# Two transformer blocks on one core: the order of products and adds in the second feed-forward, and the place of the modulation in the first

## The chip, the core and the metric

The kernel runs on one core of a Trainium2 chip. The metric is the device time of one execution in microseconds (us); where several executions were timed, their median. Engines are named as the profile names them: PE is TensorE (PEld its weight loads), DVE is VectorE, ACT is ScalarE, POOL is GpSimd, and SP is SyncE, which issues most of the DMAs.

## What is computed

A first transformer block (three kinds of attention, then a feed-forward) is followed by a second block whose two halves are modulated by a condition vector `c`. All tensors are float32, with 1024 tokens and a width of 1024. Of the reference these lines matter here:

```python
# first block, its second half
h = rmsnorm(x, g_mlp[l])
hid = jnp.square(jax.nn.relu(jnp.einsum("bsd,df->bsf", h, w_mlp_in[l])))
x = x + jnp.einsum("bsf,fd->bsd", hid, w_mlp_out[l])
# and, at its end, rmsnorm(x, g_final)

# second block
c_act = jax.nn.silu(c)
mod = c_act @ w_ada[l] + b_ada[l]                       # 1024 x 6144
sh1, sc1, gt1, sh2, sc2, gt2 = jnp.split(mod, 6, axis=-1)
h = _modulate(_rmsnorm(x, g_mix[l]), sh1, sc1)
x = x + gt1 * _mixer(h, ...)
h = _modulate(_rmsnorm(x, g_ffn[l]), sh2, sc2)
a = jnp.square(jax.nn.relu(jnp.einsum('bsd,df->bsf', h, w_ff1[l])))
x = x + gt2 * jnp.einsum('bsf,fd->bsd', a, w_ff2[l])
# and rmsnorm(x, g_final_2)
```

## The kernel before, in words

Each engine has its own program, written out by hand in the order in which it runs; semaphores join them. Nothing is scheduled by a planner. A float32 product is made of three matmuls on parts that were split into a high and a low half: high by high, high by low, low by high.

**The two feed-forwards.** The function `ff(0)` is the feed-forward of the first block and `ff(1)` that of the second; on each engine both are one piece of code, with `k` = 0 or 1. Each of the two matrix products of a feed-forward is done by a Strassen-Winograd scheme with seven half-size products, numbered 1 to 7.

- The **hidden phase** runs over the list `SEQ`: 16 units of the hidden width, seven products each, so 112 in all, each of twelve matmuls of 128x512 (PE lines 2523 to 2525). ACT splits the weights into their high part and DVE makes the low part (L1783), DVE also sums finished products (L1824), POOL makes the sums of weights and hidden tiles, and SP writes the finished hidden units to DRAM (`hidden_out`).
- The **output phase** runs over the list `STEPS`: 56 steps, 8 for each of the seven products in the order `ORDER2` = 1, 2, 5, 6, 3, 7, 4, with 24 matmuls a step (PE lines 2549 to 2551). For each step SP loads an operand from the hidden scratch (`a_load`) and one from the weights (`b_load`), ACT makes their high parts (L1245, L1250) and DVE their low parts (`step_lo`, L1931 and L1934) in rings of three buffers; for products 5, 6, 7 and 4 POOL first makes a difference of two weight tiles (`ff_b_sums`, L817). Products 1, 6, 7 and 4 add up in PSUM banks 0 to 3 and products 2, 5 and 3 in banks 4 to 7. One step after a product is complete, DVE's `evict` adds its four banks onto `xs`, the residual. In `ff(1)` each bank is first multiplied by the gate row `rowv` into `gained_sum` (L1885) and then added (L1889). PE waits, bank by bank, for the adds of a product before it writes its bank anew. From the loop's steps 3 to 10 SP also reloads `xs` from a scratch, one 512 KB piece a step; the last hidden unit is written at step 6 of SP's loop, and `a_load(7)` waits for that write to have landed, since it reads it back.

**The modulation** (`mod` above) is done beside the hidden phase of `ff(0)`. `w_ada` is cut into 96 "rows", pieces of 128x512 (256 KB). SP loads them in turn into two buffers `ada` (`ada_load`, L515), DVE multiplies each by a column of `c_act` and adds it into `ada_sum` (`modulation`, L1834 for the first of eight and L1836 for the other seven), and PE reduces every eight rows over partitions by four matmuls with a single column (`modulation`, L2490), into bank 4. The table `ADA_OPS` sets eight rows beside every eight products, from product 8 on. PE has one such group every eight products, from product 17 on: twelve in all. Since `ada_sum` is one tile, DVE's first row of a group waits for PE's matmuls on the group before. After the hidden phase DVE adds `b_ada` to the 48 columns (`modc`), makes the factors `1 + scale` (`amod`), and POOL writes 16 of the columns to a scratch (`mod_d`), from which two gate rows are read back later.

What the change touches: the table `ADA_OPS`; in the SP program `ff_loads`; in the POOL program `ff_b_sums`, the load of the row `g_final` into `rowv`, and the two writes to `mod_d`; in the DVE program `modulation`, `evict` and `ff`; in the PE program `modulation` and the loop over `STEPS` in `ff`.

## Time and profile before

| what | us |
|---|---|
| median of 3 executions (lowest, highest) | 2747.98 (2745.04, 2748.63) |
| profiled execution, its own time | 2745.53 |
| span of its trace | 2742.5 |
| PE busy | 2508.6 (91% of the span) |
| DVE busy | 1585.7 (58%) |
| ACT busy | 1214.5 (44%) |
| POOL busy | 837.7 (31%) |

The page gives the busy time of each engine and a granted TensorE clock, 0.966 of full speed as a mean over the span. Matmuls are pipelined: a row of PE shows a length of some 0.39 us, while one starts every 0.23 us, so times on PE are best read from starts. A row of the timeline is start, duration, engine, line, operation, what it writes from what it reads, the shape, and in brackets the idle time of that engine just before it with what ended it. In the rows and diffs below, `NS` is 56 and `NP` is 112.

### The profile page before, as it was taken

The page shows a single profiled execution, that of the slowest core. Times are in us where ns is not written, and L with a number is a line of the kernel's source. Part 1 is how long each engine was busy: PE and PEld are TensorE (multiplying, and loading weights), DVE is VectorE, ACT ScalarE, POOL GpSimd, SP SyncE. Part 2 cuts the span into 40 slices and gives each one's busy share as a digit, 9 for nine tenths or more (in the row PEclk, how much of TensorE's full clock was granted, in tenths as well). Part 3 has the DMA queues.
Part 4 walks back from the last instruction along what each step waited for, and adds up shares of the span by engine and source line. Part 5 has one row for each costly group of instructions (what it writes and reads, how often), then busy time and mean ns, then how long its engine had stood idle before and what let it go on. Part 6 is the DMA issues. An engine that isn't in the chain of part 4 may idle for free.

```text
span 2742.5 us, 32784 instructions
## 1 busy us (share of the span) xinstructions
PE 2508.6 (91%) x11852; PEld 2037.8 (74%) x11852; DVE 1585.7 (58%) x2796; ACT 1214.5 (44%) x2236; POOL 837.7 (31%) x740
## 2 busy tenths in 40 slices
PE   4997899997899799999999979988698999999997
PEld 4765778885678677777888867867586888877885
DVE  5357459875463787875545843335647444355675
ACT  6146357736312644444434443225426555543343
POOL 0222422231110355653333300004003655515142
PEclk9999999999999999999999989999798999999998
DMA  4102123334152267768755422122332444495444
GB/s 156 44 20 76 43 68 97 95 102 154 46 190 103 89 202 218 228 216 256 280 161 163 140 86 92 63 77 71 107 131 89 146 150 159 142 335 172 136 154 138
DMA packets 190128, 369.77 MB, mean 135 GB/s; under 512 B 13692, under 2 KB 58372, under 8 KB 189716
## 3 DMA queue, kind: packets, MB, share of 16 engines
q1 hardware_dynamic: 177620, 340.46, 37.8%
q10 hardware_dynamic: 8064, 14.68, 1.4%
q0 software_dynamic: 4288, 12.60, 1.4%
q8 instruction: 91, 1.49, 0.2%
q14 instruction: 65, 0.53, 0.1%
HBM read 266.95 MB, written 100.74 MB: 134 GB/s over the span
## 4 chain that ended last, share of the span: by engine, by line
PE 73%; DVE 11%; DMA 6%; ACT 5%; issue 3%; POOL 2%; SPq 0%; DVEq 0%; ACTq 0%; POOLq 0%
PE bank L2180 9%; PE bank L2181 9%; PE bank L2182 9%; PE bank L2549 7%; PE bank L2550 7%; PE bank L2551 7%; PE bank L2523 5%; PE bank L2525 5%; PE bank L2524 5%; DMA ada<-in_w_ada 3%; DVE ada_sum L1836 2%; PE bank L2357 1%; PE bank L2358 1%; PE bank L2359 1%; PE bank L2277 1%
## 5 line engine op out<-in xcount | busy, mean ns | idle before, releaser
L2523 PE MATMUL bank<-hq_hi,wq_hi 128*128 128x512 f32 x896 | 354.2, 395 | 17.6 <-DVE hq_lo L1844 11.1
L2549 PE MATMUL bank<-ring_b_hi,ring_a_hi 128*128 128x512 f32 x896 | 352.7, 394 | 13.6 <-DVE xs L1889 8.1
L2525 PE MATMUL bank<-hq_hi,wq_lo 128*128 128x512 f32 x896 | 352.4, 393 | 0.0
L2524 PE MATMUL bank<-hq_lo,wq_hi 128*128 128x512 f32 x896 | 352.0, 393 | 0.0
L2550 PE MATMUL bank<-ring_b_lo,ring_a_hi 128*128 128x512 f32 x896 | 351.5, 392 | 0.0
L2551 PE MATMUL bank<-ring_b_hi,ring_a_lo 128*128 128x512 f32 x896 | 351.3, 392 | 0.0
L1931 DVE TENSOR_TENSOR ring_a_lo<-a_raw,ring_a_hi 128x1024 fp32r<-128x1024 f32 x112 | 146.3, 1306 | 235.1 <-ACT ring_a_hi L1245 234.9
L1245 ACT ACTIVATE ring_a_hi<-a_raw 128x1024 fp32r<-128x1024 f32 x112 | 118.7, 1060 | 342.1 <-PE bank L2551 324.1
L2523 PEld LDWEIGHTS bank<-hq_hi,wq_hi 128*128 128x128 f32 x896 | 170.0, 190 | 58.0 <-DVE hq_lo L1844 16.5
L1783 DVE TENSOR_TENSOR wq_lo<-unit_raw,wq_hi 128x512 fp32r<-128x512 f32 x160 | 159.2, 1000 | 89.0 <-ACT wq_hi L1111 86.7
L2549 PEld LDWEIGHTS bank<-ring_b_hi,ring_a_hi 128*128 128x128 f32 x896 | 169.8, 189 | 53.8 <-DVE xs L1889 7.1
L2525 PEld LDWEIGHTS bank<-hq_hi,wq_lo 128*128 128x128 f32 x896 | 170.2, 190 | 36.2
L2551 PEld LDWEIGHTS bank<-ring_b_hi,ring_a_lo 128*128 128x128 f32 x896 | 169.9, 190 | 35.6
L2524 PEld LDWEIGHTS bank<-hq_lo,wq_hi 128*128 128x128 f32 x896 | 170.1, 190 | 34.9
L2550 PEld LDWEIGHTS bank<-ring_b_lo,ring_a_hi 128*128 128x128 f32 x896 | 169.9, 190 | 34.9
L1111 ACT ACTIVATE wq_hi<-unit_raw 128x512 fp32r<-128x512 f32 x160 | 99.7, 627 | 150.7 <-PE bank L2525 103.4
L817 POOL TENSOR_TENSOR chain_b<-b_raw,chain_b 128x1024 f32<-128x1024 f32 x32 | 92.0, 2876 | 215.8 <-DMA b_raw<-in_w_ff 115.9
L901 ACT ACTIVATE w_hi<-w_raw 128x512 fp32r<-128x512 f32 (+3 forms) x184 | 105.2, 604 | 98.6 <-DMA w_raw<-in_w_in 30.2
L722 POOL TENSOR_TENSOR w_lo<-w_raw,w_hi 128x512 fp32r<-128x512 f32 x56 | 74.8, 1344 | 227.4 <-ACT w_hi L901 223.1
L1418 DVE TENSOR_TENSOR w_lo<-w_raw,w_hi 128x512 fp32r<-128x512 f32 (+3 forms) x128 | 78.5, 649 | 88.9 <-ACT w_hi L901 87.3
L2180 PE MATMUL bank<-h_hi,w_hi 128*128 128x512 f32 (+1 forms) x288 | 113.3, 393 | 10.1 <-ACT qhT L1336 10.1
L1177 ACT ACTIVATE part<-bank 128x512 f32<-128x512 f32 x90 | 53.8, 598 | 154.2 <-PE bank L2525 154.2
(452 smaller groups left out, 5784.0 us busy)
## 6 DMA issues: line engine op xcount, KB each, us to landing
a_raw<-hidden_scratch SPq DMA_DIRECT2D x112, 512.0 KB, 3.4
hidden_scratch<-hidden SPq DMA_DIRECT2D x32, 1024.0 KB, 5.1
w_raw<-in_w_in SPq DMA_DIRECT2D x104, 256.0 KB, 2.8
ada<-in_w_ada SPq DMA_DIRECT2D x96, 256.0 KB, 3.0
hidden_scratch<-hidden SPq DMA_DIRECT2D x32, 768.0 KB, 4.8
unit_raw<-in_w_mlp_in SPq DMA_DIRECT2D x16, 1024.0 KB, 8.4
b_raw<-in_w_mlp_out SPq DMA_DIRECT2D x32, 512.0 KB, 4.6
unit_raw<-in_w_ff SPq DMA_DIRECT2D x16, 1024.0 KB, 5.3
```

The costliest lines, as they stand in the source:

```text
L1245: A_(ra_hi[s % 3][:, :, :], a_raw[raw_slot(s)][:, :, :], ACT.Copy).then_inc(a_hi.sem, 1)
L1783: tt(wq[p][1][:, :, :], unit_operand(p, u), wq[p][0][:, :, :].bitcast(f32), ALU.subtract).then_inc(wq_lo.sem, 1)
L1931: tt(ra_lo[r][:, :, :], a_raw[raw_slot(s)][:, :, :], ra_hi[r][:, :, :].bitcast(f32), ALU.subtract)\
L2180: mm(out, lh, rh, start=(i == 0), stop=False)
L2181: mm(out, lh, rl, start=False, stop=False)
L2182: last = mm(out, ll, rh, start=False, stop=(i == n - 1))
L2523: mm(o, lh[:, q, :], rh[:, q, :], start=(fresh and q == 0), stop=False, skip_group_check=True)
L2524: mm(o, lh[:, q, :], rl[:, q, :], start=False, stop=False, skip_group_check=True)
L2525: l = mm(o, ll[:, q, :], rh[:, q, :], start=False, stop=(q == 3), skip_group_check=True)
L2549: mm(o, ra_hi[r][:, e, js], rb_hi[r][:, e, :], start=(fresh and v == 0 and e == 0), stop=False, skip_group_check=True)
L2550: mm(o, ra_hi[r][:, e, js], rb_lo[r][:, e, :], start=False, stop=False, skip_group_check=True)
L2551: l = mm(o, ra_lo[r][:, e, js], rb_hi[r][:, e, :], start=False, stop=end, skip_group_check=True)
```

## The change

**1. Rows of the modulation.** Of the 96 rows 32 stay beside the first hidden phase, one every three products, with four groups on PE (after products 33, 57, 81 and 105). The other 64 go to steps 3 to 39 of the output phase of `ff(0)`, two in most steps and one in every third or fourth; they are added up in eight tiles `ada_kept` of their own, so no late row waits for PE. SP issues their loads between `b_load` and the reload of `xs`, four steps ahead of DVE's loop. The eight late groups on PE stand at the heads of steps 44 to 51, into bank 7, the first behind a wait for the eviction of product 3. The columns come in two parts: `mod_columns(0)` after the hidden phase, `mod_columns(1)` after step 52.

**2. POOL's order.** The load of `g_final` into `rowv` moves from before all sums of weight tiles to before the one for step 43; the two writes to `mod_d` move from before these sums to behind them.

**3. The gate products.** In `ff(1)` `evict` does the four gate products of a product first and then the four adds. PE's wait for the banks in `ff(1)` is on the gate product (a new semaphore `f_gt`) and no longer on the add.

```diff
-        ADA_AT = (0, 1, 1, 1, 2, 1, 1, 1)
-        ADA_OPS = {}
-        for m in range(8, 104):
-            n, j = (m - 8) // 8, m % 8
-            ADA_OPS[m] = [8 * n + sum(ADA_AT[:j]) + i for i in range(ADA_AT[j])]
+        ADA_EARLY = 32
+        ADA_OPS = {8 + 3 * r: [r] for r in range(ADA_EARLY)}
+        ADA_LATE = {}
+        for r in range(ADA_EARLY, 96):
+            ADA_LATE.setdefault(3 + (r - ADA_EARLY) * 37 // 64, []).append(r)
...
                     a_load(s)
                     b_load(s)
+                    if k == 0:
+                        for r in ADA_LATE.get(s - 4, ()):
+                            if r + 2 < 96:
+                                ada_load(r + 2)
                     if 3 <= s < 11:
...
-            def ff_b_sums(k):
+            def ff_b_sums(k, at=None, extra=None):
...
+                        if s == at:
+                            extra()
...
             ff_sums(0)
-            pool.wait_ge(ada_s, 96)
-            row(rowv, a["g_final"].rearrange("(o n) -> o n", o=1))
-            pool.wait_ge(ada_ok, 1)
+            ff_b_sums(0, STEP[7, 3], gain_row)
+            pool.wait_ge(ada_ok, 2)
             with nc.allow_non_contiguous_dma(reason="two rows of the modulation, from columns"):
                 for k in (16, 40):
                     pool.dma_start(mod_d[k:k + 8, :].rearrange("k p -> p k"), modc[:, k:k + 8]).then_inc(mod_out, 16)
-            ff_b_sums(0)
...
                 n, kk = r // 8, r % 8
                 x = adab[r % 2][:, :]
+                o = (adac if r < ADA_EARLY else adak[n - ADA_EARLY // 8])[:, :]
                 dve.wait_ge(ada_in[r % 2], 16 * (r // 2 + 1))
                 if kk == 0:
-                    if n:
+                    if 0 < n < ADA_EARLY // 8:
                         dve.wait_ge(ada_mm, n)
...
-            def evict(k, o, j):
+            def evict(k, o):
 
                 p = ORDER2[o]
                 h, n = TARGET[p]
-                x, b = xs[:, 4 * h + j, 512 * n:512 * n + 512], sum_bank(p, j)[:, :]
-                sum_ready(k, o, j)
                 if k:
-                    link(tt(gained_sum[j][:, :], b, rowv[:, 512 * n:512 * n + 512], ALU.mult))
-                    b = gained_sum[j][:, :]
-                if o:
-                    dve.wait_ge(ev.sem, ev.base + 28 * k + 4 * o - 4 + j + 1)
-                tt(x, x, b, ALU.add).then_inc(ev.sem, 1)
+                    for j in range(4):
+                        sum_ready(k, o, j)
+                        tt(gained_sum[j][:, :], sum_bank(p, j)[:, :], rowv[:, 512 * n:512 * n + 512], ALU.mult)\
+                            .then_inc(f_gt.sem, 1)
+                for j in range(4):
+                    x, b = xs[:, 4 * h + j, 512 * n:512 * n + 512], gained_sum[j] if k else sum_bank(p, j)
+                    if k:
+                        dve.wait_ge(f_gt.sem, f_gt.base + 4 * o + j + 1)
+                    else:
+                        sum_ready(k, o, j)
+                    if o:
+                        dve.wait_ge(ev.sem, ev.base + 28 * k + 4 * o - 4 + j + 1)
+                    tt(x, x, b[:, :], ALU.add).then_inc(ev.sem, 1)
...
+                    mod_columns(0)
+                    dve.wait_ge(made.sem, made.base + NP)
                 for s in range(2, NS):
                     step_lo(k, s)
+                    if k == 0:
+                        for r in ADA_LATE.get(s, ()):
+                            modulation(r)
+                        if s == 52:
+                            mod_columns(1)
                     if s >= 8 and s % 8 == 1:
...
-                    if k == 0 and m % 8 == 1 and m >= 17:
-                        modulation((m - 17) // 8)
+                    if k == 0 and m in (33, 57, 81, 105):
+                        modulation((m - 33) // 24)
...
+                    if k == 0 and s >= 44 and s < 52:
+                        if s == 44:
+                            pe.wait_ge(ev.sem, ev.base + 20)
+                        modulation(s - 40)
+                    if k == 0 and s == 54:
+                        pe.wait_ge(ada_ok, 2)
...
                             if v == 0 and e == 0 and oi >= 2:
-                                pe.wait_ge(ev.sem, ev.base + 28 * k + 4 * {5: 1, 6: 0, 3: 2, 7: 3, 4: 5}[p] + j + 1)
+                                read = f_gt.base if k else ev.base
+                                pe.wait_ge((f_gt if k else ev).sem, read + 4 * {5: 1, 6: 0, 3: 2, 7: 3, 4: 5}[p] + j + 1)
```

Three places of the new order follow. First DVE in the hidden phase of `ff(0)`, where `wq_lo` are low parts of weights, `hidden` are sums of finished products and `ada_sum` is a row of the modulation. Before:

```order
L1834 TENSOR_SCALAR ada_sum<-ada_158,cact 128x512
L1783 TENSOR_TENSOR wq_lo<-unit_raw_195,wq_hi 128x512
L1836 SCALAR_TENSOR_TENSOR ada_sum<-ada_159,cact,ada_sum 128x512
L1824 TENSOR_TENSOR hidden_215<-bank,part_219 128x512
L1783 TENSOR_TENSOR wq_lo<-wsum_193,wq_hi 128x512
L1836 SCALAR_TENSOR_TENSOR ada_sum<-ada_158,cact,ada_sum 128x512
```

And now:

```order
L1846 TENSOR_SCALAR ada_sum<-ada_158,cact 128x512
L1794 TENSOR_TENSOR wq_lo<-wsum_202,wq_hi 128x512
L1794 TENSOR_TENSOR wq_lo<-unit_raw_203,wq_hi 128x512
L1835 TENSOR_TENSOR hidden_223<-bank,part_227 128x512
L1794 TENSOR_TENSOR wq_lo<-wsum_201,wq_hi 128x512
L1848 SCALAR_TENSOR_TENSOR ada_sum<-ada_159,cact,ada_sum 128x512
```

Where three rows stood among three other operations, two now stand among four, and further on one among three or more. Second SP's issues at steps 6 to 8 of the first output phase as they are now (`hidden_scratch` is the last hidden unit on its way out, `a_raw` and `chain_b` or `b_raw` the operands of a step, `ada` a row of the modulation, `xs` the residual):

```order
L503 DMA hidden_scratch<-hidden_223 128x3x512
L503 DMA hidden_scratch<-hidden_223 128x4x512
L558 DMA a_raw_249<-hidden_scratch 128x1024
L577 DMA chain_b<-in_w_mlp_out 128x2x512
L595 DMA xs<-residual_scratch 128x1024
L558 DMA a_raw_250<-hidden_scratch 128x1024
L577 DMA chain_b<-in_w_mlp_out 128x2x512
L516 DMA ada_158<-in_w_ada 128x512
L516 DMA ada_159<-in_w_ada 128x512
L595 DMA xs<-residual_scratch 128x1024
```

The two loads of `ada` are new here: they are rows 34 and 35, and they stand behind the second `a_raw`, which is `a_load(7)`. Third DVE's eviction of one product in `ff(1)`. Before:

```order
L1885 TENSOR_TENSOR gained_sum_223<-bank,rowv 128x512
L1889 TENSOR_TENSOR xs<-xs,gained_sum_223 128x512
L1885 TENSOR_TENSOR gained_sum_224<-bank,rowv 128x512
L1889 TENSOR_TENSOR xs<-xs,gained_sum_224 128x512
L1885 TENSOR_TENSOR gained_sum_225<-bank,rowv 128x512
L1889 TENSOR_TENSOR xs<-xs,gained_sum_225 128x512
L1885 TENSOR_TENSOR gained_sum_226<-bank,rowv 128x512
L1889 TENSOR_TENSOR xs<-xs,gained_sum_226 128x512
```

And now:

```order
L1897 TENSOR_TENSOR gained_sum_231<-bank,rowv 128x512
L1897 TENSOR_TENSOR gained_sum_232<-bank,rowv 128x512
L1897 TENSOR_TENSOR gained_sum_233<-bank,rowv 128x512
L1897 TENSOR_TENSOR gained_sum_234<-bank,rowv 128x512
L1907 TENSOR_TENSOR xs<-xs,gained_sum_231 128x512
L1907 TENSOR_TENSOR xs<-xs,gained_sum_232 128x512
L1907 TENSOR_TENSOR xs<-xs,gained_sum_233 128x512
L1907 TENSOR_TENSOR xs<-xs,gained_sum_234 128x512
```

The instructions are the same eight; the four that read the banks now stand together at the front.

## Rows read from the trace of the kernel before

**Rows 1.** Page, chain that ended last: shares of the span by line.
```profile
PE bank L2180 9%; PE bank L2181 9%; PE bank L2182 9%; PE bank L2549 7%; PE bank L2550 7%; PE bank L2551 7%; PE bank L2523 5%; PE bank L2525 5%; PE bank L2524 5%; DMA ada<-in_w_ada 3%; DVE ada_sum L1836 2%; PE bank L2357 1%; PE bank L2358 1%; PE bank L2359 1%; PE bank L2277 1%
```

**Rows 2.** Timeline of PE: the same place of `ff(0)` and of `ff(1)`.
```profile
944.32 0.47 PE L2523 MATMUL bank<-hq_hi,wq_hi 128*128 128x512 f32 x1 [0.78 <-ACT hidden L1177]
...
1267.63 0.39 PE L2549 MATMUL bank<-ring_b_hi,ring_a_hi 128*128 128x512 f32 x1
...
2109.16 0.47 PE L2523 MATMUL bank<-hq_hi,wq_hi 128*128 128x512 f32 x1 [0.78 <-ACT hidden L1177]
...
2401.97 0.47 PE L2549 MATMUL bank<-ring_b_hi,ring_a_hi 128*128 128x512 f32 x1 [0.43 <-DVE ring_b_lo L1934]
```

**Rows 3.** Waits of PE, 940 to 1250 us: total, times, longest.
```profile
PE bank L2490 <- DVE ada_sum L1836: 13.2, 10, 2.0
```

**Rows 4.** One window: us, busy (count) of PE, PEld, DVE, ACT, POOL; clock, DMA, GB/s.
```profile
1000.00:1020.00 20.00, 18.00 (x77) 14.61 (x76) 14.53 (x16) 8.06 (x14) 11.47 (x8) 0.91 0.69 221
```

**Rows 5.** Timeline of PE, one group of the modulation.
```profile
1249.30 0.95 PE L2490 MATMUL bank<-one,ada_sum 128*128 128x1 f32 x8
1250.11 0.49 PE L2523 MATMUL bank<-hq_hi,wq_hi 128*128 128x512 f32 x1
```

**Rows 6.** Timeline of ACT, second output phase: high parts of steps' operands.
```profile
2493.85 1.06 ACT L1245 ACTIVATE ring_a_hi<-a_raw 128x1024 fp32r<-128x1024 f32 x1 [3.43 <-PE bank L2551]
...
2505.46 1.06 ACT L1245 ACTIVATE ring_a_hi<-a_raw 128x1024 fp32r<-128x1024 f32 x1 [9.60 <-PE bank L2551]
...
2674.11 1.06 ACT L1245 ACTIVATE ring_a_hi<-a_raw 128x1024 fp32r<-128x1024 f32 x1 [3.43 <-PE bank L2551]
...
2688.97 1.06 ACT L1245 ACTIVATE ring_a_hi<-a_raw 128x1024 fp32r<-128x1024 f32 x1 [11.37 <-PE bank L2551]
```

**Rows 7.** Timeline of POOL and DVE beside the first of these gaps.
```profile
2490.67 3.45 POOL L817 TENSOR_TENSOR chain_b<-b_raw,chain_b 128x1024 f32<-128x1024 f32 x1 [1.99 <-DMA b_raw<-in_w_ff]
...
2491.82 0.69 DVE L1885 TENSOR_TENSOR gained_sum<-bank,rowv 128x512 f32<-128x512 f32 x1
2492.54 2.13 DVE L1889 TENSOR_TENSOR xs<-xs,gained_sum 128x512 f32<-128x512 f32 x1
```

**Rows 8.** Timeline of DVE, first gate product before the second gap.
```profile
2673.80 0.68 DVE L1885 TENSOR_TENSOR gained_sum<-bank,rowv 128x512 f32<-128x512 f32 x1
```

**Rows 9.** Timeline of DVE and ACT at the end of the program.
```profile
2725.76 0.69 DVE L1889 TENSOR_TENSOR xs<-xs,gained_sum 128x512 f32<-128x512 f32 x1
...
2730.47 1.06 ACT L1125 ACTIVATE junk_second<-xs 128x1024 f32<-128x1024 f32 x1 [0.18 <-DVE xs L1889]
```

**Rows 10.** DMA issues at 2416.26, 2425.56, 1281.6 and 1283.8 us: KB, us to landing.
```profile
hidden_scratch<-hidden SPq DMA_DIRECT2D x1, 1024.0 KB, 8.9
...
chain_b<-in_w_ff SPq DMA_DIRECT2D x1, 512.0 KB, 6.9
...
hidden_scratch<-hidden SPq DMA_DIRECT2D x1, 1024.0 KB, 15.8
...
mod_scratch<-modc POOLq DMA_DIRECT2D x1, 4.0 KB, 16.9
```

**Rows 11.** Timeline of ACT, high part of step 7's operand in `ff(1)`.
```profile
2434.01 1.06 ACT L1245 ACTIVATE ring_a_hi<-a_raw 128x1024 fp32r<-128x1024 f32 x1 [3.43 <-PE bank L2551]
```

**Rows 12.** Timeline of DVE: low part of a step's operand, and two rows of the modulation.
```profile
2419.93 1.22 DVE L1934 TENSOR_TENSOR ring_b_lo<-chain_b,ring_b_hi 128x1024 fp32r<-128x1024 f32 x1
...
1001.40 1.77 DVE L1836 SCALAR_TENSOR_TENSOR ada_sum<-ada,cact,ada_sum 128x512 f32<-128x512 f32 x1
...
1019.33 0.74 DVE L1836 SCALAR_TENSOR_TENSOR ada_sum<-ada,cact,ada_sum 128x512 f32<-128x512 f32 x1
```

**Rows 13.** Timeline of POOL, a difference of weight tiles with DVE idle beside it.
```profile
1464.90 2.40 POOL L817 TENSOR_TENSOR b_raw<-kept_b,b_raw 128x1024 f32<-128x1024 f32 x1 [47.19 <-DMA b_raw<-in_w_mlp_out]
```

**Rows 14.** DMA from 2395 to 2485 us, GB/s in 40 slices.
```profile
GB/s 281 401 401 403 399 409 397 406 397 404 286 324 401 398 330 293 355 419 410 410 395 404 401 353 330 154 0 249 253 327 125 287 157 205 244 74 267 150 232 222
```

**Rows 15.** Page, DMA issues: KB each, median us to landing.
```profile
ada<-in_w_ada SPq DMA_DIRECT2D x96, 256.0 KB, 3.0
```

More of the change, by code:

```diff
@@ L168, in build @@
         adac = at("ada_sum", [P, 512], f32, 30720)
+        adak = [at(f"ada_kept{i}", [P, 512], f32, 40960 + 2048 * i) for i in range(8)]
         mT = [act_pair("mT0", s2), act_pair("mT1", s3)]
@@ L817, in ff_b_sums, with gain_row @@
                         nc.gpsimd.tensor_tensor(o, x, y, ALU.subtract).then_inc(b_s.sem, 1)
+            def gain_row():
+                pool.wait_ge(ada_s, 96)
+                row(rowv, a["g_final"].rearrange("(o n) -> o n", o=1))
             ff_sums(0)
-            pool.wait_ge(ada_s, 96)
-            row(rowv, a["g_final"].rearrange("(o n) -> o n", o=1))
-            pool.wait_ge(ada_ok, 1)
+            ff_b_sums(0, STEP[7, 3], gain_row)
+            pool.wait_ge(ada_ok, 2)
             with nc.allow_non_contiguous_dma(reason="two rows of the modulation, from columns"):
@@ L1267, in _ @@
             act.wait_ge(b_lo.sem, b_lo.base + NS)
+            act.wait_ge(ada_mm, 12)
             norm_mod_hi(24, 0, 0, 0, range(4))
@@ L1909, in ff @@
                 if k == 0:
-                    dve.wait_ge(ada_mm, 12)
-                    tt(modc[:, :], bank[4][:, 0:48], cols[:, c_ada:c_ada + 48], ALU.add).then_inc(ada_ok, 1)
-                    dve.wait_ge(ada_ok, 1)
-                    for i, (g, sc) in enumerate(((c_gmix2, 8), (c_gffn2, 32))):
-                        link(tsc(amod[:, 8 * i:8 * i + 8], modc[:, sc:sc + 8], 1.0, None, ALU.add))
-                        link(tt(amod[:, 8 * i:8 * i + 8], amod[:, 8 * i:8 * i + 8], cols[:, g:g + 8], ALU.mult))
+                    mod_columns(0)
+                    dve.wait_ge(made.sem, made.base + NP)
                 for s in range(2, NS):
                     step_lo(k, s)
+                    if k == 0:
[3 more added lines that the diff above has]
+                            mod_columns(1)
                     if s >= 8 and s % 8 == 1:
@@ L1922, in ff, with mod_columns @@
                             dve.wait_ge(row_in, 16 * 3)
-                        for j in range(4):
-                            evict(k, s // 8 - 1, j)
+                        evict(k, s // 8 - 1)
                     beside(s)
+            def mod_columns(i):
+                x, c0, c1 = (bank[4], 0, 16) if i == 0 else (bank[7], 16, 48)
+                dve.wait_ge(ada_mm, 12 if i else 4)
+                tt(modc[:, c0:c1], x[:, c0:c1], cols[:, c_ada + c0:c_ada + c1], ALU.add).then_inc(ada_ok, 1)
+                dve.wait_ge(ada_ok, i + 1)
+                g, sc = ((c_gmix2, 8), (c_gffn2, 32))[i]
+                link(tsc(amod[:, 8 * i:8 * i + 8], modc[:, sc:sc + 8], 1.0, None, ALU.add))
+                link(tt(amod[:, 8 * i:8 * i + 8], amod[:, 8 * i:8 * i + 8], cols[:, g:g + 8], ALU.mult))
             def step_lo(k, s):
@@ L1972, in _ @@
             norm_mod_lo(24, range(4, 8))
-            for j in range(4):
-                evict(0, 6, j)
+            evict(0, 6)
             split_lo(C_V, 1, range(4, 8))
@@ L2163, in _ @@
             ff(1, last_first_half)
-            for j in range(4):
-                evict(1, 6, j)
+            evict(1, 6)
             half_rstd(9, 1)
@@ L2486, in modulation @@
             def modulation(n):
+                early = n < ADA_EARLY // 8
+                src, dst = (adac, bank[4]) if early else (adak[n - ADA_EARLY // 8], bank[7])
                 pe.wait_ge(ada_s, 8 * n + 8)
                 for e in range(4):
-                    l = mm(bank[4][:, 4 * n + e:4 * n + e + 1], adac[:, e * P:(e + 1) * P], one[:, :], start=True, stop=True)
+                    l = mm(dst[:, 4 * n + e:4 * n + e + 1], src[:, e * P:(e + 1) * P], one[:, :], start=True, stop=True)
                 l.then_inc(ada_mm, 1)
```

8 lines of the change are left out of this document (4 added, 4 removed).

## The prediction
> **What bounds the kernel now.** I read the page first, then the timeline of PE at four places, and then the waits there. The chain of waits that ended last runs mostly through PE, and beside the products' lines it names two things that are not products: the load of the modulation's rows with 3% and DVE's scaled adds with 2% [rows 1]. The chain tells where to look, not what is to be won. For that the kernel has a control of its own: `ff(1)` runs the same hidden phase as `ff(0)` without the modulation. From the same product to the first matmul of the output phase, PE needs 1267.63 - 944.32 = 323.3 us in `ff(0)` and 2401.97 - 2109.16 = 292.8 us in `ff(1)` [rows 2]. So the modulation costs the first hidden phase 30.5 us. Of these, 13.2 us are PE's waits for `ada_sum` [rows 3]; one group holds PE from 1249.30 to 1250.11, 0.81 us [rows 5], so twelve groups take 9.7 us; in one stretch of waits the granted clock shows as 0.91 [rows 4], against a mean of 0.966 over the span; this and small delays behind it are the remaining 7.6 us.
>
> The second place is the output phase of `ff(1)`. ACT starts the high part of an operand after PE has freed a slot of the ring, so its starts show PE's pace. A start with the usual 3.43 us of idle time before it stands at 2493.85, the next one at 2505.46 after 9.60 us of idle time [rows 6]. The excess is 9.60 - 3.43 = 6.17 us, and the usual pitch is 11.61 - 6.17 = 5.44 us. At the other place, 2674.11 to 2688.97, the pitch is 14.86 us, an excess of 9.42 us [rows 6]. Both are where PE turns to banks of an earlier product and waits for the adds. One sees why: the gate product takes 0.69 us although a sum of POOL runs beside it from 2490.67 for 3.45 us, but the add behind it takes 2.13 us and ends just after that sum [rows 7]. Each bank comes free after product and add, while PE needs a new bank every 0.68 us (three matmuls of 0.227 us, a step's 5.44 us over 24).
>
> **The change, part by part.** *Rows beside the hidden phase.* 64 of 96 rows leave it, and eight of twelve groups. With one row every three products DVE has a whole product's time and more for each, and the next row of a group is due 24 products after the last, so I expect the waits for `ada_sum` to go entirely. Four groups of 0.81 us [rows 5] stay, 3.2 us of the 30.5. **-27.3 us.** The other 32 rows stay hidden as DVE's other work is in `ff(1)`.
>
> *Groups on PE in the output phase.* Eight groups at the heads of steps 44 to 51, where PE is the bound: 8 x 0.81 [rows 5] = **+6.5 us**. Their sums are done by step 39, and the wait for product 3's eviction is met a few steps before step 44, so neither adds a wait.
>
> *Gate products ahead.* Products read a bank and one tile in SBUF, and at 0.68 us [rows 8] they come at PE's pace. The adds no longer stand before PE. At the second place the first product starts only at 2673.80 [rows 8], about when PE wants that bank, so one product's 0.7 us stays: 6.17 + 9.42 - 0.7 = **-14.9 us**. Behind the adds on DVE stand the next step's low parts, which are late by at most the four adds, and the ring covers them: a high part starts two steps, 10.9 us, ahead of PE's need.
>
> *The end.* The last eviction is on the path, since no PE work hides it. Before, the first add starts at 2725.76, after one product, and the last of ACT's four row sums at 2730.47 [rows 9]. Now the first add stands behind three more products, 3 x 0.69 = 2.1 us later; from then on ACT's sums follow at 1.06 us and 0.18 us of idle time [rows 9], 1.24 at most, where before they followed the pairs on DVE. The last sum starts at about 2726.5 + 2.1 + 3 x 1.24 = 2732.3 at most, 1.8 us later; with 1.06 a sum it would be 1.3. I take **+1.5 us**.
>
> *First late rows.* The late rows stand in order on DVE between low parts. Row 34, at step 4, is loaded behind `a_load(7)`, and this waits for the last hidden unit's write to land. In `ff(1)`, at the same place, the write is issued at 2416.26 and lands 8.9 us later, and the next `b_load` at 2425.56 takes 6.9 us [rows 10]. A gain row of 512 KB stood ahead of that write, 1.3 us at 401 GB/s [rows 14], and is gone in the new order of `ff(0)`. So row 34 lands some 2431.8 and row 35 0.7 us later (256 KB at 401 GB/s); behind them come two scaled adds at 0.75 and the low parts of step 5 at 1.22 each, so 2435.6 on this clock, where PE wants them at 2434.0, the start of step 7's high part, which marks the end of step 4 [rows 11, 12]. **+2 us**. Bounds: 0 if the write lands early; 9 if it lands 15.8 us after issue as in `ff(0)` before, 6.9 later than I assume [rows 10]. There, the scattered writes to `mod_scratch` were under way at the same time and took 16.9 us [rows 10]; they have moved away, so I stay near the first.
>
> *An eviction behind rows.* At step 17 of `ff(0)` the eviction stands behind row 57 and beside a sum of POOL of 2.40 us [rows 13], while PE waits for banks 4 to 7. A scaled add takes 0.74 us alone and 1.77 us elsewhere [rows 12]. **+2 us**, between 0 and 4 (a row of 1.77 and one sum).
>
> *POOL's order.* `rowv` and the scattered writes leave the start of the output phase: 0, since PE does not wait there for POOL. `g_final` is needed at DVE's step 45, two steps after it is issued or more, and 512 KB took 6.9 us [rows 10]: 0; uncovered it would cost the rest of that time. The scattered writes now run at the end of `ff(0)` beside the next projection's weight loads: 0, at most +4, if they hold these loads as long as the write above was held. `mod_columns(1)`, four short operations at step 52, is needed at step 54: 0. DVE's new wait for product 112 was met by the operation before it: 0.
>
> The sum is -27.3 + 6.5 - 14.9 + 1.5 + 2 + 2 = **-30.2 us**. Against the profiled execution's 2745.53 that is 2715.3; the median of the runs lies 2.45 above that execution, so I expect **2717.7, rounded 2718 us**, 1.1% faster.
>
> What the loads do in steps 3 to 10 bears on the +2. In a step there are 512 KB of each operand, 512 KB of `xs` and 1.73 rows of 256 KB, 2.03 MB in 5.44 us or 372 GB/s; the rows of this place reach 397 to 419 GB/s in most slices [rows 14], so it fits. The Trainium skill's page "DMA: Bandwidth & Descriptors", section "Where 436 GB/s comes from", bounds a core's traffic with HBM at some 358 GB/s; by that figure a step would last 5.66 us, an estimate of 8 x 0.22 = 1.8 us more. The trace speaks against it with 401 GB/s and more over 50 us.
>
> **The rivals.** *R1: DVE and POOL bound the middle of the first output phase.* Where scaled adds and POOL's sums exclude each other, a step of products 5 and 6 takes 2 x 1.22 for low parts, 1.73 x 0.75 for rows and 2.40 for the sum [rows 12, 13], 6.1 us, and 6.5 with an eighth of an eviction's four adds, against PE's 5.44. Over 16 steps that is 11 to 17 us, less a lead of about 6 (10.9 less the 4.6 of two high and two low parts). It would put 5 to 10.5 in the place of the +2: 2721 to 2726. For it: 1.77 against 0.74 [rows 12], and the add of 2.13 [rows 7]. Against it: low parts take 1.22 us also beside POOL's sums, and the sum can run while DVE waits for ACT. The Trainium skill has this as a rule, on the page "SBUF — State Buffer", section "Who interferes with whom": a DVE instruction with two inputs in SBUF and a GpSimd one that reads SBUF shut each other out for their whole length. By that rule the low parts would be shut out too, which makes R1 likelier; the stretched add agrees with it.
>
> *R2: the first late rows come as late as their bound*, +9 for +2: 2725. *R3: the second stall of `ff(1)` stays*, because something else than the adds, such as the late first product, holds PE there: +8.7, 2726.
>
> *R4, slower than before: the round trip of two buffers.* DVE waits in order for each row; a buffer is loaded again only when its row is added. 64 rows in two buffers are 32 round trips of t in a row, to fit in 37 steps x 5.44 = 201 us. With a load of 6.9 us, as beside `xs` [rows 10], 0.75 for the add and some 0.7 for the issue, t is 8.35 and the chain 267 us; less the lead of 6, PE would be 60 us late, against 34.2 won elsewhere (30.2 and the two terms of 2 that this contains): 2748 + 26 = 2774. It decides from t = 7.7 on, (201 + 6 + 34.2 + 5.5) / 32. For it: landings at the start of an output phase are 7 to 16 us [rows 10]. Against it: rows landed in 3.0 us in the median [rows 15], and behind step 10 the `xs` loads are gone.
>
> *R5: the 30.5 us are not the modulation's.* `ff(0)` and `ff(1)` have other weights and other neighbours; if all of it stays, the time is 2745, no change.
>
> **How the numbers follow.** The forecast has 0.66, R1 0.14, R2 0.09, R3 0.06, R4 0.02 and R5 0.03. A measurement of this kernel can tell 0.2%, 5.5 us, from no change. Forecast and R1 to R3 are all faster: 0.95; R5 is the same: 0.03; R4 is slower: 0.02. The range goes down to 2711: the two terms of 2 at nothing, the 0.7 of the second stall gone, the end at 1.3, and 1.8 for the spread of the runs (half of 3.6). It goes up to 2733: first rows at 9 and the eviction's stretch at R1's 10.5 together would be 2733. R4 and R5 are left out, with what remains beyond these ends.
>
> **What would show it.** Right: PE from the same product to the output phase in about 296 us; four groups there, with no wait for `ada_sum`; one short wait of DVE for `ada` at step 4; starts of ACT at the usual 5.44 us around steps 16 and 48 of `ff(1)`; the last row sum 1.5 us later behind the last matmul. Wrong: a pitch over 5.44 us through steps 13 to 29 of `ff(0)` (R1), waits of PE for low parts that add up in steps 3 to 39 with DVE idle on `ada` (R4), or a gap of some 9 us that stays near step 48 of `ff(1)` (R3).

## The result, and the profile after

The changed kernel takes 2732.94 us in the median (2729.03 to 2734.04), the kernel before 2747.94 in the same runs: a ratio of 0.9946, with a 95% interval of 0.9933 to 0.9959. It is faster by 15 us where the forecast had 30, at the upper edge of the range, and clear of the 0.2% that can be told from nothing. The direction and the sign of every part were right; half of the gain is missing.

The profiled execution has a span of 2728.9 us, 13.6 less than before. Where that comes from is read by cutting the span at PE's own work: in each phase from the first to the last start of a high-by-high matmul (L2551 and L2584 now), in us.

| stretch | before | after | difference | forecast |
|---|---|---|---|---|
| up to the first product of `ff(0)` | 920.13 | 922.55 | +2.4 | 0 |
| hidden phase of `ff(0)` | 346.82 | 319.19 | -27.6 | -27.3 |
| output phase of `ff(0)` | 310.27 | 336.08 | **+25.8** | **+10.5** |
| between the feed-forwards | 506.03 | 505.65 | -0.4 | 0 |
| hidden phase of `ff(1)` | 316.77 | 316.88 | +0.1 | 0 |
| output phase of `ff(1)` | 324.23 | 308.63 | -15.6 | -14.9 |
| from there to the end | 16.30 | 17.94 | +1.6 | +1.5 |

The 2.4 us ahead of the first product lie in code that the change does not touch; all later kernels have 922 to 925 us there, also those in which nothing ahead of the output phase of `ff(1)` differs from the kernel before. So one line carries the miss: the first output phase.

First what came as forecast. The chain of waits of the changed kernel, shares by line, answers to [rows 1]; the scaled adds' share fell from 2% to 1%, the rows' loads kept their 3%:

```profile
PE bank L2206 9%; PE bank L2207 9%; PE bank L2208 9%; PE bank L2551 7%; PE bank L2553 7%; PE bank L2552 7%; PE bank L2584 6%; PE bank L2586 6%; PE bank L2585 6%; DMA ada<-in_w_ada 3%; DVE ada_kept L1848 1%; PE bank L2383 1%; PE bank L2384 1%; PE bank L2385 1%; PE bank L2303 1%
```

The timeline of PE at the two places of `ff(0)` that [rows 2] show for the kernel before:

```profile
946.38 0.47 PE L2551 MATMUL bank<-hq_hi,wq_hi 128*128 128x512 f32 x1 [0.78 <-ACT hidden L1187]
...
1242.42 0.39 PE L2584 MATMUL bank<-ring_b_hi,ring_a_hi 128*128 128x512 f32 x1
```

1242.42 - 946.38 = 296.0 us, the "about 296" that the prediction named. PE's waits in this stretch (940 to 1242 us) are these, and `ada_sum` [rows 3] is not among them:

```profile
PE bank L2551 <- ACT hidden L1187: 2.0, 2, 1.2
PE bank L2551 <- ACT part L1187: 0.8, 1, 0.8
```

In the output phase of `ff(1)` ACT's starts, which had pitches of 11.61 and 14.86 us [rows 6], run through the first place at 5.44, and PE waits no more for adds. First ACT around step 16, then all of PE's waits from 2402 to 2711 us, the place around step 48 included:

```profile
2488.80 1.06 ACT L1255 ACTIVATE ring_a_hi<-a_raw 128x1024 fp32r<-128x1024 f32 x1 [3.43 <-PE bank L2586]
2494.24 1.06 ACT L1255 ACTIVATE ring_a_hi<-a_raw 128x1024 fp32r<-128x1024 f32 x1 [3.43 <-PE bank L2586]
2499.68 1.06 ACT L1255 ACTIVATE ring_a_hi<-a_raw 128x1024 fp32r<-128x1024 f32 x1 [3.43 <-PE bank L2586]
```

```profile
PE bank L2584 <- DVE hidden L1835: 2.6, 1, 2.6
PE bank L2584 <- DVE ring_b_lo L1962: 0.5, 1, 0.5
```

And the end: the four products stand ahead of the four adds, and ACT's last row sum starts 1.24 us behind the one before, limited by ACT itself (the last two of four; the small instruction between them reads the sum out). [rows 9] show the same place before.

```profile
2709.80 2.73 DVE L1897 TENSOR_TENSOR gained_sum<-bank,rowv 128x512 f32<-128x512 f32 x4 [6.22 <-PE bank L2586]
2712.45 2.49 DVE L1907 TENSOR_TENSOR xs<-xs,gained_sum 128x512 f32<-128x512 f32 x4
```

```profile
2715.64 1.06 ACT L1135 ACTIVATE junk_second<-xs 128x1024 f32<-128x1024 f32 x1
2716.61 0.19 ACT L1135 ACTIVATION_READ_ACCUMULATOR junk_second<-xs 128x1 f32 x1
2716.88 1.06 ACT L1135 ACTIVATE junk_second<-xs 128x1024 f32<-128x1024 f32 x1
```

Now the first output phase. PE's waits in it (1242 to 1579 us) in the changed kernel; before there was the one for `hidden` alone, 2.4 us:

```profile
PE bank L2584 <- DVE xs L1907: 7.4, 1, 7.4
PE bank L2584 <- DVE ring_b_lo L1962: 5.7, 4, 2.0
PE bank L2584 <- DVE hidden L1835: 2.6, 1, 2.6
```

and those of DVE in the same stretch:

```profile
DVE ada_kept L1848 <- DMA ada<-in_w_ada: 31.8, 19, 9.3
DVE ring_a_lo L1959 <- ACT ring_a_hi L1255: 29.8, 19, 3.1
...
DVE ada_kept L1846 <- DMA ada<-in_w_ada: 2.2, 2, 1.5
```

DVE waits 34 us for rows, at 21 places, where the prediction expected one short wait at step 4. PE's pace, taken from every second step's first matmul, departs from 10.88 us a pair at these places: 1.9 us in the first two steps, 0.9 at step 5, 1.8 at step 10, 1.6 at step 14, 9.6 at step 16 and behind it, 2.2 at step 28, and 0.955 a step at steps 44 to 51, 7.6 in all. Together that is 25.6 of the 25.8 us. The largest is read best in time. DVE around the eviction of step 17, which PE needs for its step 16:

```profile
1337.18 2.36 DVE L1848 SCALAR_TENSOR_TENSOR ada_kept<-ada,cact,ada_kept 128x512 f32<-128x512 f32 x1 [0.66 <-DMA ada<-in_w_ada]
1339.58 0.49 DVE L1846 TENSOR_SCALAR ada_kept<-ada,cact 128x512 f32<-128x512 f32 x1
1340.10 1.23 DVE L1959 TENSOR_TENSOR ring_a_lo<-a_raw,ring_a_hi 128x1024 fp32r<-128x1024 f32 x1
1341.24 1.22 DVE L1962 TENSOR_TENSOR ring_b_lo<-chain_b,ring_b_hi 128x1024 fp32r<-128x1024 f32 x1
1343.38 1.83 DVE L1848 SCALAR_TENSOR_TENSOR ada_kept<-ada,cact,ada_kept 128x512 f32<-128x512 f32 x1 [0.92 <-DMA ada<-in_w_ada]
1345.24 2.48 DVE L1907 TENSOR_TENSOR xs<-xs,bank 128x512 f32<-128x512 f32 x4
```

POOL beside it, PE's first matmul of step 16, and the load of row 57 (issued at 1339.57; KB, us to landing):

```profile
1336.61 2.39 POOL L824 TENSOR_TENSOR chain_b<-b_raw,chain_b 128x1024 f32<-128x1024 f32 x1 [3.03 <-DMA b_raw<-in_w_mlp_out]
1341.34 3.32 POOL L824 TENSOR_TENSOR chain_b<-b_raw,chain_b 128x1024 f32<-128x1024 f32 x1 [2.34 <-DMA b_raw<-in_w_mlp_out]
```

```profile
1346.08 0.77 PE L2584 MATMUL bank<-ring_b_hi,ring_a_hi 128*128 128x512 f32 x1 [7.35 <-DVE xs L1907]
```

```profile
ada<-in_w_ada SPq DMA_DIRECT2D x1, 256.0 KB, 3.8
```

Row 55 waits for its load (0.66 us) and is then stretched by a sum of POOL to 2.36 us, against 0.74 alone [rows 12]. Its end at 1339.54 lets SP issue row 57 into the same buffer at 1339.57; that lands at 1343.37, and DVE takes it at 1343.38. Row 57 is stretched to 1.83 by the next sum. Only then comes the eviction, at 1345.24, where PE had finished step 15 at 1338.7. PE loses 7.35 us, and its next matmuls run 0.43 us apart for some 4 us in place of 0.23: the granted clock is 0.50, the lower of its two levels (1.2 GHz of 2.4), from 1346 to 1350 us, and 0.98 over the next 5 us. From 1319.7 us to this eviction DVE is idle for rows alone and never for an operand of a step. So operands that came late, by POOL's sums or because SP stands in order behind the adds too, are not what made DVE late here.

The three smaller stalls are not all alike. At steps 14 and 28 a row comes late (DVE idle for 2.55 and 2.15 us), scaled adds are stretched, and the last delay is a low part that waits for one of POOL's sums, 3.4 us in place of 1.22. POOL, DVE and PE at step 14:

```profile
1322.97 3.36 POOL L824 TENSOR_TENSOR chain_b<-b_raw,chain_b 128x1024 f32<-128x1024 f32 x1 [1.48 <-DMA b_raw<-in_w_mlp_out]
1324.01 3.41 DVE L1962 TENSOR_TENSOR ring_b_lo<-b_raw,ring_b_hi 128x1024 fp32r<-128x1024 f32 x1
1327.56 0.47 PE L2584 MATMUL bank<-ring_b_hi,ring_a_hi 128*128 128x512 f32 x1 [1.48 <-DVE ring_b_lo L1962]
```

The kernel before has such low parts too, for example

```profile
1512.42 2.79 POOL L817 TENSOR_TENSOR chain_b<-b_raw,chain_b 128x1024 f32<-128x1024 f32 x1 [2.24 <-DMA b_raw<-in_w_mlp_out]
1512.88 3.41 DVE L1934 TENSOR_TENSOR ring_b_lo<-b_raw,ring_b_hi 128x1024 fp32r<-128x1024 f32 x1
```

At step 10 no sum is near, for POOL is idle from 1256.6 to 1319.1 us: there the eviction of step 9 stands behind a row for which DVE waited 1.59 us.

### The profile page after: what moved, and what is told of

Read it like the earlier page. It is cut to its first block, busy times and chain, and to the rows that moved or that the text cites. A ratio compares the mean times of both kernels' runs of the same rounds, so it can differ in the third digit from the quotient of the medians.

```text
span 2728.9 us, 32790 instructions
## 1 busy us (share of the span) xinstructions
PE 2503.4 (92%) x11852; PEld 2038.2 (75%) x11852; DVE 1575.0 (58%) x2797; ACT 1213.4 (44%) x2236; POOL 824.7 (30%) x740
## 4 chain that ended last, share of the span: by engine, by line
PE 75%; DVE 9%; DMA 6%; ACT 5%; issue 3%; POOL 2%; SPq 0%; DVEq 0%; ACTq 0%; POOLq 0%
PE bank L2206 9%; PE bank L2207 9%; PE bank L2208 9%; PE bank L2551 7%; PE bank L2553 7%; PE bank L2552 7%; PE bank L2584 6%; PE bank L2586 6%; PE bank L2585 6%; DMA ada<-in_w_ada 3%; DVE ada_kept L1848 1%; PE bank L2383 1%; PE bank L2384 1%; PE bank L2385 1%; PE bank L2303 1%
## 5 line engine op out<-in xcount | busy, mean ns | idle before, releaser
L2584 PE MATMUL bank<-ring_b_hi,ring_a_hi 128*128 128x512 f32 x896 | 352.5, 393 | 18.8 <-DVE xs L1907 7.4
L2551 PE MATMUL bank<-hq_hi,wq_hi 128*128 128x512 f32 x896 | 351.8, 393 | 18.8 <-DVE hq_lo L1856 12.4
L1959 DVE TENSOR_TENSOR ring_a_lo<-a_raw,ring_a_hi 128x1024 fp32r<-128x1024 f32 x112 | 153.0, 1366 | 130.8 <-ACT ring_a_hi L1255 129.7
L1794 DVE TENSOR_TENSOR wq_lo<-unit_raw,wq_hi 128x512 fp32r<-128x512 f32 x160 | 149.0, 936 | 126.5 <-ACT wq_hi L1121 124.5
L2551 PEld LDWEIGHTS bank<-hq_hi,wq_hi 128*128 128x128 f32 x896 | 169.2, 189 | 57.7 <-DVE hq_lo L1856 18.0
L2584 PEld LDWEIGHTS bank<-ring_b_hi,ring_a_hi 128*128 128x128 f32 x896 | 169.6, 189 | 57.0 <-issue 16.2
L911 ACT ACTIVATE w_hi<-w_raw 128x512 fp32r<-128x512 f32 (+3 forms) x184 | 105.4, 604 | 97.4 <-DMA w_raw<-in_w_in 30.5
```

The lines of the kernel that those rows point to most:

```text
L1794: tt(wq[p][1][:, :, :], unit_operand(p, u), wq[p][0][:, :, :].bitcast(f32), ALU.subtract).then_inc(wq_lo.sem, 1)
L1959: tt(ra_lo[r][:, :, :], a_raw[raw_slot(s)][:, :, :], ra_hi[r][:, :, :].bitcast(f32), ALU.subtract)\
L2551: mm(o, lh[:, q, :], rh[:, q, :], start=(fresh and q == 0), stop=False, skip_group_check=True)
L2584: mm(o, ra_hi[r][:, e, js], rb_hi[r][:, e, :], start=(fresh and v == 0 and e == 0), stop=False, skip_group_check=True)
```

## The experiments

Two theories stood after the result. **A, the round trip**: with two buffers, row r + 2 is loaded only behind the add of row r, so DVE, which works in order, is held to the loads and has no lead over PE. **B, exclusion**: DVE's instructions with two inputs in SBUF and POOL's sums hold each other up, and that costs PE the time by itself (the prediction's R1). Each ratio is to executions of the kernel before that were timed beside the kernel (their medians were 2746.86 to 2747.94). The phase is the output phase of `ff(0)`, from one trace of each kernel; its excess over the 310.27 us of the kernel before is split at PE's steps: the first six, those behind them, and, in kernels that have them there, the groups of steps 44 to 51 at 7.64. All in us.

| kernel | phase | steps 0 to 5 | steps 6 to 43 | end | median | ratio [95%] |
|---|---|---|---|---|---|---|
| before | 310.27 | 0 | 0 | 16.30 | 2747.94 | 1 |
| changed | 336.08 | 2.7 | 15.4 | 17.94 | 2732.94 | 0.9946 [0.9933, 0.9959] |
| gates_only | 311.63 | 1.4 | 0.0 | 18.00 | 2733.46 | 0.9959 [0.9944, 0.9973] |
| rows_only | 331.59 | 4.2 | 9.5 | 16.31 | 2741.02 | 0.9983 [0.9974, 0.9993] |
| pool_order | 310.23 | 0.0 | 0.0 | 16.30 | 2745.64 | 0.9998 [0.9986, 1.0010] |
| deep_rows | 323.49 | 2.6 | 3.0 | 17.98 | 2721.56 | 0.9913 [0.9896, 0.9930] |
| short_sums | 323.36 | 4.2 | 1.2 | 17.95 | 2720.52 | 0.9913 [0.9894, 0.9932] |
| deep_short | 320.33 | 2.5 | 0.0 | 17.95 | 2715.32, one execution | |
| skip_evictions | 330.68 | 4.3 | 8.5 | 17.99 | 2723.06 | 0.9911 [0.9896, 0.9927] |
| rows_planned | 320.56 | 1.6 | 1.1 | 16.29 | 2717.52 | 0.9884 [0.9868, 0.9900] |
| no_late_groups | 311.22 | 0.0 | 1.0, no groups | 16.28 | 2703.02 | 0.9837 [0.9815, 0.9858] |

**The parts alone.** `gates_only` is the kernel before with the new `evict` and PE's wait on `f_gt`:

> The kernel before with the third part of the change alone: four gate products ahead of four adds, and PE's wait on the product. The changed kernel's trace has the second output phase 15.6 us shorter (324.2 to 308.6 from its first to its last product) and the end 1.6 us longer (16.3 to 17.9). If the parts add up, this kernel is 14 us faster than the kernel before, some 2734 us, with its first hidden and output phases as before (346.8 and 310.3 us). If instead the missing half of the gain was lost here, through adds that come late for the row sums of step 42, it is less than 10 us faster.

Measured: 0.9959, 11 us faster (7 to 15), an interval that holds 14 and does not exclude the "less than 10". The trace does, for it shows what was expected: an output phase of `ff(1)` of 308.56 us and an end of 18.00; the first hidden phase was 345.20. `rows_only` is the changed kernel with the old eviction:

> The changed kernel with the old eviction (product and add in turn, PE's wait on the add), so parts one and two of the change alone. If the parts add up, the first hidden phase gains 27.6 us and the first output phase loses 25.8: no change that can be measured, 2745 to 2749 us. My forecast of these two parts was -27.3 + 10.5 = -16.8 us, 2731 us: that would put the loss elsewhere.

Measured: 0.9983, 5 us faster (2 to 7) and 4 under the 2745 to 2749 expected, with 319.40 and 331.59 us for the first feed-forward: of the 27.6 us won some 21 are given back at once. Its first feed-forward is the changed kernel's, instruction for instruction, so the 4.5 us between 331.59 and 336.08 show how far the stalls differ from one execution to another (9.5 against 15.4 behind step 5). Its output phase of `ff(1)`, with the old eviction, took 320.75 us, and that of `pool_order` 321.18, against 324.23 in the trace of the kernel before. `pool_order` is the kernel before with the second part:

```diff
             ff_sums(0)
-            pool.wait_ge(ada_s, 96)
-            row(rowv, a["g_final"].rearrange("(o n) -> o n", o=1))
+            ff_b_sums(0, STEP[7, 3], gain_row)
             pool.wait_ge(ada_ok, 1)
...
-            ff_b_sums(0)
```

> The kernel before with the second part of the change alone: the load of rowv behind the first 19 of the sums of weight tiles for products 5 to 7 that it now stands among (before step 43), and the two scattered writes behind all sums. My forecast costs it at 0, +4 at most if the scattered writes hold up the loads of the next projection. First output phase 310 to 312 us, the stretch between the two feed-forwards 505 to 508 us, kernel 2744 to 2750 us; the last hidden unit's write should land in 7 to 9 us in place of 15.8.

Measured: 0.9998, no change, as costed. The last hidden unit's write landed in 7.1 us, against 15.8 before [rows 10]:

```profile
hidden_scratch<-hidden SPq DMA_DIRECT2D x1, 1024.0 KB, 7.1
```

**A against B.** `deep_rows` gives the late rows four more buffers, in weight tiles that are free by then, and `short_sums` takes POOL's sums away and leaves the buffers as they are.

```diff
+        adax = [at(f"ada_late{i}", [P, 512], f32, 57344 + 2048 * i) for i in range(4)]
...
+        ADA_ISSUE = {}
+        for r in range(ADA_EARLY + 2, 96):
+            ADA_ISSUE.setdefault(ADA_STEP[r - 6] + 5 if r >= ADA_EARLY + 6 else 7, []).append(r)
...
-                        for r in ADA_LATE.get(s - 4, ()):
-                            if r + 2 < 96:
-                                ada_load(r + 2)
+                        for r in ADA_ISSUE.get(s, ()):
+                            ada_load(r)
```

```diff
+                        if k == 0 and p in (5, 6):
+                            o, x, y = o[:, :, 0:16], x[:, :, 0:16], y[:, :, 0:16]
                         nc.gpsimd.tensor_tensor(o, x, y, ALU.subtract).then_inc(b_s.sem, 1)
```

> The changed kernel with six buffers for the late rows in place of two, so that a row's load is issued some two to three steps ahead of its add and no longer behind the add of the row two before. Nothing else moves, and the first late rows are still issued behind step 7's operands. Theory A, the round trip: DVE waits 34 us for rows in steps 3 to 39, in order, so it has no lead left, and each meeting with a sum of POOL or an eviction reaches PE. By A DVE's waits for rows fall to a few us at the start, the first output phase goes from 336.1 to 316 to 321 us, and the kernel is at 2713 to 2718 us. Theory B, exclusion alone: scaled adds and low parts that stand still beside POOL's sums cost PE the time whether DVE waits for rows or not; by B the phase stays above 328 us, and the kernel above 2725 us.

> The changed kernel with POOL's sums for products 5 and 6 of the first output phase cut to 16 of 512 columns (the rest of each weight tile is left unsubtracted, so the first block's feed-forward is not computed in full). Two buffers and all waits for rows stay. By theory B (exclusion alone) the stalls of PE beside these sums go, 9.4 us at the eviction of step 17, 1.6 and 2.1 us at two other steps: 13 us, some 2720 us. By theory A (no lead because of the round trip) the waits for rows stay, and with them the stretch in which PE follows DVE; the scaled adds are shorter, so part of it goes: 4 to 9 us, 2724 to 2729 us.

Measured: both bring the phase to about 323.4 us and both kernels to 0.9913. The stalls behind step 5, 9.5 to 15.4 us with both causes there, fall to 3.0 with more buffers and to 1.2 without the sums. So A and B each had a part of it right. For `deep_rows` A's figures were missed by 2.5 us in the phase, about what the first late rows and the clock cost in steps 0 to 5, and by 3.6 in the median; B's "above 328" fell. For `short_sums` it was B's figure that came, although DVE's waits for rows were nearly all still there (31.0 us, 34.0 in the changed kernel), so behind step 5 the waits alone cost PE next to nothing. DVE's longest waits for rows in the phase, of `deep_rows` (13.2 us with the shorter ones) and then of `short_sums`:

```profile
DVE ada_kept L1865 <- DMA ada_late<-in_w_ada: 11.3, 2, 9.3
```

```profile
DVE ada_kept L1850 <- DMA ada<-in_w_ada: 28.6, 19, 9.7
```

In `deep_rows` the scaled adds are still stretched, and the eviction of step 17 again stands behind one, but it starts far earlier against PE, whose wait there is 2.8 us in place of 7.35:

```profile
1333.16 2.61 POOL L840 TENSOR_TENSOR chain_b<-b_raw,chain_b 128x1024 f32<-128x1024 f32 x1 [3.08 <-DMA b_raw<-in_w_mlp_out]
```

```profile
1333.47 2.85 DVE L1865 SCALAR_TENSOR_TENSOR ada_kept<-ada,cact,ada_kept 128x512 f32<-128x512 f32 x1
1336.35 2.48 DVE L1924 TENSOR_TENSOR xs<-xs,bank 128x512 f32<-128x512 f32 x4
```

`deep_short` takes both away:

> Six buffers for the late rows, and POOL's sums for products 5 and 6 of the first output phase cut to 16 of 512 columns (the rest is left unsubtracted). Each alone brought the first output phase from 336.1 to about 323.4 us. If the two causes are needed together for the loss (a DVE without lead, and meetings with POOL), both at once give little more than one: 318 to 322 us, the floor being 310.3 + 8 groups at 0.955 = 317.9. If they were two separate losses, both would have to add, 336 - 25 = 311 us, which is under that floor.

Measured: 320.33 us, 3.1 below either alone, and nothing is left behind step 5. Most of the stalls needs both causes: with both there are 9.5 to 15.4 us of it, with one 1.2 or 3.0, with none 0.0. These are single traces, and two of the same code differed by 6 us; but the ratios of `deep_rows` and `short_sums`, 0.9913 both against 0.9946 of the changed kernel, say the same.

**The place.** `skip_evictions` has the changed kernel's two buffers and all of POOL's sums, but no row at the two steps ahead of the evictions of steps 17 and 25:

```diff
-            ADA_LATE.setdefault(3 + (r - ADA_EARLY) * 37 // 64, []).append(r)
+            ADA_LATE.setdefault(ADA_PLAN[r - ADA_EARLY], []).append(r)
```

> The changed kernel with another table for the late rows: the same steps 3 to 39 and the same two buffers, but no row at steps 16, 17, 24 and 25, so that DVE has two steps without rows ahead of the evictions of steps 17 and 25. If the 9.4 us at step 17 come from DVE's arriving there without a lead (theory A), two free steps give some 3 us of lead back and the stall falls to 0 to 3 us: first output phase 327 to 331 us, kernel 2723 to 2728 us. If the eviction's adds themselves are what is slow beside POOL, it stays at 6 us or more.

Measured: 330.68 us for the phase and 0.9911 for the kernel. PE's wait at the eviction fell to 3.5 us, from 7.35 in the changed kernel and 7.0 in `rows_only`. The matmuls behind it were slow as before, so 6.3 us are left of the 9.4 to 9.6 that count this too: by its number that is the second branch. Its reason is not the one that the branch gives, for the four adds took 2.47 us, as in the changed kernel. The low part of step 17 ahead of them, beside a sum of POOL, took 3.41 us in place of 1.22. So DVE still arrived late, and with no row at these two steps a low part was enough for it. A wait of 2.0 us stood at step 14, and the 8.5 us in all are hardly below the 9.5 of `rows_only`. The median is better than that by more than this phase explains. As a cure this is inconclusive.

**A faster version.** `rows_planned` joins what was learnt: six buffers, the first four late rows issued ahead of the last hidden unit's write, no rows ahead of the two evictions, fewer beside POOL's sums and three a step in steps 32 to 36; and the very last eviction as product and add in turn.

> An attempt at a faster version: the changed kernel with six buffers, the first four late rows issued at SP's step 5 ahead of the last hidden unit's write, no row at steps 16, 17, 24 and 25, one row in most steps of products 5 and 6, three in steps 32 to 36; and the very last eviction again as product and add in turn. By theory A the 0.8 us at step 5 and the 3 us at step 17 of the kernel with six buffers go (first output phase 318 to 320 us) and the end is 1.6 us shorter (16.3 us): 2721.6 - 3.8 - 1.6 = 2716 us, between 2714 and 2719.

Measured: 0.9884 (0.9868 to 0.9900), 32 us under the kernel before by the ratio, 30 by the medians, and faster than the changed one. Its first output phase is 320.56 us, with no wait left at step 5, 0.87 us at the eviction of step 17 and no other wait for DVE behind the first steps; its end is back at 16.29.

**The groups' price.** `no_late_groups` is this version without the eight late groups on PE:

```diff
                 pe.wait_ge(ada_s, 8 * n + 8)
+                if not early:
+                    pe.sem_inc(ada_mm, 1)
+                    return
```

> The faster version with the eight late groups on PE left out (so columns 16 to 47 of the modulation are not made, and the second block's gates, shift and scale are not the right ones); all loads, scaled adds and waits stay. The pitch of steps 44 to 51 is 6.395 us in the traces, 0.955 above the usual 5.44, so the groups cost 8 x 0.955 = 7.6 us of the first output phase: 320.6 should become 312.9 us, 2710 us for the kernel. By my forecast's price, 0.81 a group as in the hidden phase, it would be 6.5 us: 314.1 us.

Measured: 311.22 us, 9.3 less. 1.6 of that is a shorter slow stretch in the first two steps (13.57 us for them against 15.13); of the other 7.8 the groups' pitch is 7.64, 0.955 each as expected, and the rest a slightly shorter stall at step 16. A group holds PE for 0.81 us from its start to the next matmul, as in the hidden phase [rows 5], but that next one is also 0.32 us ahead of its successor in place of 0.23:

```profile
1502.71 0.94 PE L2518 MATMUL bank<-one,ada_kept 128*128 128x1 f32 x8
1503.52 0.49 PE L2584 MATMUL bank<-ring_b_hi,ring_a_hi 128*128 128x512 f32 x1
1503.84 0.40 PE L2585 MATMUL bank<-ring_b_lo,ring_a_hi 128*128 128x512 f32 x1
```

The kernel's median, 7 us under the expected 2710, fell by 14.5 us against that of `rows_planned`, more than the 9.3 of the phase; the two were not timed side by side. The profiled spans fell by 9.6 (2715.7 to 2706.1). The rest is not explained here.

## Why the prediction was half right

- **Rows beside the hidden phase, -27.3**: right; 27.6, and PE's waits for `ada_sum` went entirely. The control by `ff(1)` gave the size to 1%, and that this is closer than executions agree is luck: with the old rows the phase took 345.2 to 346.8 us in three traces. The rival that the 30.5 us were not the modulation's fell.
- **Gate products ahead, -14.9**: right; 15.6 against the trace from which the forecast was made. Against the two other traces with the old eviction it is 12.1 and 12.6, so some 3 us of the 14.9 belonged to that one execution. R3 fell; even the 0.7 us left for the second place is not seen as a wait.
- **The end, +1.5**: right, 1.6; the last version took it back.
- **POOL's order, 0**: right; 0.9998 alone.
- **First late rows, +2**: right in kind. In the changed kernel 0.9 us are lost at step 5, because PE had come there 1.9 us late; in the four kernels with late rows behind `a_load(7)` where it had not, 2.4 us (`deep_short`) to 4.2 and 4.3, a wait of some 2.2 to 2.4 and in three of them a slow stretch behind it. Issuing four rows earlier (`rows_planned`) took the wait away.
- **Groups on PE, +6.5**: mis-sized; 7.6. The group was priced by the next matmul's start, without the slower start behind it.
- **An eviction behind rows, +2, between 0 and 4**: this is the step that failed. It measured 9.6 at that place, and three smaller stalls, 5.6 us, had been costed at nothing: 15.2 us against 2. Two of the three, 3.8 us at steps 14 and 28, are of the same kind; the 1.8 us at step 10 have no sum of POOL beside them. The term priced one row of 1.77 us and one sum, from an eviction that begins on time. It took DVE's lead over PE as given (the 6 us of R1 and R4), while the order of SP's issues takes it away: row r + 2 is issued when row r is added.

  The prediction had both halves, as rivals apart from each other. R4 asked only whether 32 round trips fit into 201 us; they did, so it cost the round trip at nothing, though with two rows a step a trip has to fit into one step of 5.44 us, and the one from the end of row 55's add to that of row 57's took 5.67. R1 had the stretched adds, and counted on the lead to take 6 us of them; its upper bound of 10.5 was passed too, in this trace, by 13.4 us at steps 14, 16 and 28. And R1 was argued down by a reading that does not hold, that low parts take 1.22 us also beside POOL's sums. The 1.22 of [rows 12] has no such sum beside it; a low part that starts ahead of a sum takes 1.22, but one that starts behind it took up to 3.4 us, so at steps 14 and 28 and already in the kernel before.

  The round trip and the exclusion together make the stalls, and the stalls make the miss: a stretched add passes its delay on to the load two rows later, and through it to the next add, as from row 55 to row 57 to the eviction above. The runs show that either cause without the other is worth 1 to 3 us.
- What remains are 1.9 us in the first two steps, where the granted clock falls to some 0.7 over 5 us behind PE's wait for `hidden`. Of the eleven executions traced, four show it (15.0 to 15.5 us for two steps against 13.5 to 13.6), `gates_only` among them, which has no rows in this phase: it is not the rows' doing.
- The doubt about DMA bandwidth was settled by the trace: 366 GB/s on average from 1245 to 1300 us in the changed kernel, 386 in `rows_planned`, with the DMA engines busy throughout (shares of 1.00 and 1.03). The bound of 358 GB/s that the Trainium skill's page "DMA: Bandwidth & Descriptors" gives in "Where 436 GB/s comes from" did not hold here.
- Scaled adds and low parts, with two inputs in SBUF, end some 0.5 to 1.1 us after the sum that they wait for (the add of row 55 at 1339.54, the sum at 1339.00), while the gate products, with one input in PSUM, ran beside a sum at 0.69 us [rows 7]. This bears out the Trainium skill's page "SBUF — State Buffer", section "Who interferes with whom".

## What to carry to other kernels

Work that is put on an engine "in the shadow" has to be priced by its waits too: if it stands in order and its load is issued only behind its own predecessor, it ties the engine to the round trip, and the lead that hid everything else can be gone even while the average still fits. Check which place downstream has no slack (here the one eviction that PE needs at once), and what meets there. Two rivals that are each bearable should be costed together when they draw on the same lead; and a few more buffers, issued some steps ahead, cost nothing here and brought most of the lost gain back.

## What was not expected of the hardware

A wait of PE can cost more than its length. After 7.35 us at step 16 the matmuls ran 0.43 us apart for about 4 us, at a granted clock of 0.50, which added 2 us. The wait of 2.4 to 2.6 us for `hidden`, in the first step of the phase, was followed by such a stretch in four of the eleven executions (a granted clock of 0.66 to 0.73 over 5 us) and not in the other seven. In the output phase of `ff(1)` before, PE's waits for adds were 8.1 us in all, but the phase lost 15.6; in the two other traces with the old eviction 7.2 and 8.5 us of waits came to 12.1 and 12.6 lost. The waits row alone would have priced that part at half to two thirds.
